# Gate tiles 10 and 11 as seven half-size products before the attention, instead of a plain product after it

## The reference, cut to what matters

```python
h = _rmsnorm(x, norm_g) * (1 + scale) + shift        # 512 x 1024
q_a,k_a,v_a,z_a,q_b,k_b,v_b,z_b,f_logit,g_logit = split(h @ w_in)
y_a = (stick_breaking(q_a,k_a,v_a) * silu(z_a)) @ w_o_sb
y_b = (forgetting_attention(q_b,k_b,v_b,F) * silu(z_b)) @ w_o_fox
gates = sigmoid(g_logit + b_gate)                    # 512 x 2048, 16 tiles of 128 features
x = x + gate * ((gates[:, :D] * y_a + gates[:, D:] * y_b) @ w_out)
```

## Time and profile before

| what | value |
|---|---|
| median of 3 runs | 1242.37 us |
| the profiled execution's own time | 1242.71 us |
| its span | 1240.9 us |
| PE / DVE / ACT / POOL busy | 98% / 69% / 53% / 35% |
| granted TensorE clock | 1.00 (2.4 GHz) in every stretch looked at |

### The profile page before, as it was taken

One profiled execution on the slowest core, in us unless ns is written; L12 is line 12 of the kernel. 1 busy time (PEld: TensorE's weight loads), 2 busy tenths in 40 slices (PEclk: granted clock), 3 DMA queues, 4 the chain that ended last, 5 costly groups with the idle time before them and its releaser, 6 DMA issues.

```text
span 1240.9 us, 22894 instructions
## 1 busy us (share of the span) xinstructions
PE 1213.3 (98%) x9270; PEld 1040.5 (84%) x9270; DVE 859.1 (69%) x1342; ACT 653.8 (53%) x1028; POOL 431.4 (35%) x330
## 2 busy tenths in 40 slices
PE   6999999999999999999998989999999999999999
PEld 6798999876767877777787768788878999999999
DVE  4289897789663266596648757456668888878974
ACT  6555463777665533463446544454335555556452
POOL 5562000422333736455343035540555223333000
PEclk9999999999999999999999999999999999999999
DMA  9953332666977993766321018851542565656554
GB/s 387 360 199 125 116 107 98 245 214 222 261 197 173 249 322 112 239 150 154 91 103 37 4 69 308 260 136 24 149 125 94 162 187 187 187 170 210 185 185 143
DMA packets 42182, 215.53 MB, mean 174 GB/s; under 512 B 5080, under 2 KB 5208, under 8 KB 28128
## 3 DMA queue, kind: packets, MB, share of 16 engines
q1 hardware_dynamic: 34272, 140.74, 32.2%
q0 software_dynamic: 4608, 28.31, 12.2%
q10 hardware_dynamic: 3200, 45.04, 9.8%
HBM read 206.72 MB, written 63.98 MB: 218 GB/s over the span
## 4 chain that ended last, share of the span: by engine, by line
PE 81%; DVE 9%; ACT 4%; POOL 2%; DMA 2%; issue 2%; ACTq 0%; SPq 0%; DVEq 0%; POOLq 0%
PE banks L663 79%; PE banks L670 2%; POOL weights_low L3281 2%; DMA weights<-in_stream 2%; DVE arena L2595 1%; DVE h_low L2336 1%; ACT weights_high L1487 1%; DVE arena L2592 1%; DVE arena L2597 1%; DVE weights_low L2336 0%; DMA arena<-in_mem 0%; POOL arena L3340 0%; ACT arena L1541 0%; DVE arena L2426 0%; DVE banks L2411 0%
## 5 line engine op out<-in xcount | busy, mean ns | idle before, releaser
L3281 POOL TENSOR_TENSOR weights_low<-weights,weights_high 128x512 fp32r<-128x512 f32 (+1 forms) x216 | 310.8, 1468 | 496.5 <-ACT weights_high L1487 496.5
L663 PE MATMUL banks<-h_high_low,weights_high 128*128 128x512 f32 (+1 forms) x696 | 243.3, 350 | 1.6 <-DVE h_low L2336 1.5
L663 PE MATMUL banks<-h_low,weights_high 128*128 128x512 f32 (+1 forms) x696 | 235.8, 339 | 0.0
L663 PE MATMUL banks<-h_high_low,weights_low 128*128 128x512 f32 (+1 forms) x696 | 235.8, 339 | 0.0
L1487 ACT ACTIVATE weights_high<-weights 128x2048 fp32r<-128x2048 f32 (+2 forms) x86 | 127.0, 1489 | 73.9 <-PE banks L663 58.4
L663 PEld LDWEIGHTS banks<-h_high_low,weights_high 128*128 128x128 f32 x696 | 131.2, 188 | 21.0 <-issue 3.0
L663 PEld LDWEIGHTS banks<-h_low,weights_high 128*128 128x128 f32 x696 | 131.1, 188 | 16.5 <-issue 2.4
L663 PEld LDWEIGHTS banks<-h_high_low,weights_low 128*128 128x128 f32 x696 | 131.1, 188 | 16.1
L663 PE MATMUL banks<-arena 64*64 64x64 f32 (+6 forms) x1800 | 116.6, 263 | 1.7 <-POOL arena L3340 0.7
L663 PEld LDWEIGHTS banks<-arena 64*64 64x64 f32 (+3 forms) x1800 | 84.8, 147 | 24.1 <-issue 17.0
L3359 POOL TENSOR_TENSOR weights_low<-weights,weights_high 128x512 fp32r<-128x512 f32 x32 | 48.5, 1537 | 112.6 <-ACT weights_high L1499 112.6
(11 more groups left out here) (463 smaller groups left out, 3293.2 us busy)
## 6 DMA issues: line engine op xcount, KB each, us to landing
weights<-in_stream SPq DMA_DIRECT2D x66, 1024.0 KB, 6.1
up_sums<-in_up POOLq DMA_DIRECT2D x16, 1024.0 KB, 9.5
weights<-up_sums SPq DMA_DIRECT2D x64, 256.0 KB, 2.9
weights<-in_up SPq DMA_DIRECT2D x48, 256.0 KB, 2.9
sums_kept<-in_down POOLq DMA_DIRECT2D x16, 704.0 KB, 7.7
arena<-in_ada SPq DMA_DIRECT2D x8, 1024.0 KB, 12.0
weights<-sums_kept SPq DMA_DIRECT2D x9, 704.0 KB, 4.1
sums_kept<-in_down ACTq DMA_DIRECT2D x8, 704.0 KB, 6.2
```

The source lines that it names most:

```text
L663: ins = nc.tensor.matmul(o, lhsT, rhs, start=start, stop=stop, skip_group_check=skip)
L3281: nc.gpsimd.tensor_tensor(lo_of(c)[:, cols], raw_of(c)[:, cols], hi_of(c)[:, cols].bitcast(F32), ALU.subtract).then_inc(sem("weights_split ...
```

## The change

One more early tile, gate pair 5 (tiles 10 and 11), is put between `za` and `qb`. It is written where `kb` will be, stored in `gates_kept` by ACT two tiles later, and loaded back at fox step 4 to where `va` was. Gate tiles 12 to 15 are now copied from `GATES_AT` to `sums` on the core (the accumulators of the norms, idle then) and read from there. Each wait on `keys_kept` counts one transfer more. `project("g", ...)` after the attention has no tiles left (`EARLY_G` 10). The second chunk of `va` is done like the first: blocks 0 and 1 side by side over k. The splitting of weights after the attention is placed after gates 9, 13 and 15; the DRAM copies are issued at every second m, and four of them in the next stage; the four lows of the `a` half of `gated` move into fox steps 5, 9, 13 and 17 on DVE. TensorE waits for `MOVED0` at step 2 instead of 1, and the bank order after the attention is 2, 3, 0, 1.

```diff
-EARLY_TILES = (("qa", 1), ..., ("za", 1), ("qb", 0), ("qb", 1), ("kb", 0), ("kb", 1), ("g", 6), ("g", 7))
+EARLY_TILES = (("qa", 1), ..., ("za", 1), ("g", 5), ("qb", 0), ("qb", 1),
+               ("kb", 0), ("kb", 1), ("g", 6), ("g", 7))
-Z_FIRST, EARLY_G = EARLY_TILES.index(("za", 0)), 12
+Z_FIRST, EARLY_G = EARLY_TILES.index(("za", 0)), 10
...
+        early_gates = {5: at(8192, 2, T), 6: at(GATES_AT, 2, T), 7: at(GATES_AT + 2 * T, 2, T)}
...
+            def values_in(c, n, ready=None):
+                slot, w = next_chunk(KD, n)
+                o = [M.take(pe, ("va", c, b)) for b in range(2)]
                 for k in range(KD):
+                    split_ready(k, KD)
...
+                    for b in range(2):
+                        mm3(o[b][:, 0:n], hrow(k, b), [p_[:, k, :] for p_ in w], k == 0, k == KD - 1, ...)
...
+            values_in(1, 256, h_ready(0))
             gate_rows_in(0, ADA_RING)
-            project_rows("va", 0, NB, hrow, NB, F_WIDE)
+            values_in(0, F_WIDE)
...
-                if i == 1:
+                if i == LAG:
                     pe.wait_ge(sem("product_moved"), MOVED0)
...
-                        M.use([0, 1, 2, 3])
+                        M.use([2, 3, 0, 1])
...
# ACT, early tiles, at R7
+                    if e >= 2 and EARLY_TILES[e - 2] == ("g", 5):
+                        act.wait_ge(sem("product_moved"), early_moved(e - 2, C12))
+                        act.dma_start(gates_kept, at(8192, 2 * T)).then_inc(sem("keys_kept"), 16)
# ACT, stick steps 1 and 2
-                    act.dma_start(gates_kept, at(GATES_AT, 4 * T)).then_inc(sem("keys_kept"), 16)
+                    act.dma_start(sums.rearrange("p a b -> p (a b)"), at(GATES_AT, 4 * T)).then_inc(sem("keys_kept"), 16)
-                    act.wait_ge(sem("keys_kept"), 48)
+                    act.wait_ge(sem("keys_kept"), 64)
# ACT, fox step 4
+                if i == 4:
+                    act.dma_start(at(512 * EARLY_G, 2 * T), gates_kept).then_inc(sem("keys_kept"), 16)
# ACT, after the attention
-            act.dma_start(at(GATES_AT, 4 * T), gates_kept).then_inc(sem("keys_kept"), 16)
             for m in range(SIDE_G, EARLY_G):
                 gate_out(m)
                 gate_inverse(m)
...
             for m in range(EARLY_G, 16):
+                if m == 14:
+                    split_weights()
+                src = gates[m] if m < 12 else sums[:, m - 12, :]
...
-            for _ in range(2):
-                split_weights()
+            split_weights()
             for m in range(KD):
                 act.wait_ge(sem("merged_raw"), m + 1)
                 high(merged_hi[m], merged_raw[:, m, :], sem("merged_hi"))
-                later_copies(S2, S1, m, 2)
+                if m % 2 == 0:
+                    later_copies(S2, S1, m // 2, 2)
                 if m % 4 == 3:
                     split_weights()
             def between_blocks(k):
+                if k < DOWN_PAIRS:
+                    later_copies(S2, S1, DOWN_PAIRS + k, 2)
# DVE
+                    if EARLY_TILES[e] == ("kb", 0):
+                        dve.wait_ge(sem("keys_kept"), 48)
...
+                if i % 4 == 1 and 5 <= i <= N + 1:
+                    gated_split(i // 4 - 1)
...
-            for m in range(8):
+            for m in range(4, 8):
```

More of the change, by code:

```diff
@@ L88 @@
 EARLY_FIRST = 11
-EARLY_TILES = (("qa", 1), ("ka", 0), ("ka", 1), ("za", 0), ("za", 1), ("qb", 0), ("qb", 1), ("kb", 0), ("kb", 1), ("g", 6), ("g", 7))
+EARLY_TILES = (("qa", 1), ("ka", 0), ("ka", 1), ("za", 0), ("za", 1), ("g", 5), ("qb", 0), ("qb", 1),
+               ("kb", 0), ("kb", 1), ("g", 6), ("g", 7))
 EARLY = len(EARLY_TILES)
-Z_FIRST, EARLY_G = EARLY_TILES.index(("za", 0)), 12
+Z_FIRST, EARLY_G = EARLY_TILES.index(("za", 0)), 10
 EARLY_STEPS = [[(c, f) for c, fs in ((i, (P1, R5)), (i - 1, (Q4, P3)), (i, (R7, P6, P2))) if 0 <= c < EARLY for f in fs]
@@ L344, in build @@
         GATES_AT = 10240
-        gates = [at(512 * m if m < EARLY_G else GATES_AT + 512 * (m - EARLY_G), T) for m in range(16)]
+        gates = [at(512 * m if m < 12 else GATES_AT + 512 * (m - 12), T) for m in range(16)]
+        early_gates = {5: at(8192, 2, T), 6: at(GATES_AT, 2, T), 7: at(GATES_AT + 2 * T, 2, T)}
         merged_raw, merged_lo = at(16384, 8, T), at_r("merged_low", 16384, 8, T)
@@ L556, in early_tile @@
             if key == "g":
-                return gates[2 * c + half][:, TH * side:TH * (side + 1)]
+                return early_gates[c][:, half, TH * side:TH * (side + 1)]
             to = {"qa": qa, "ka": ka, "za": gated["a"], "qb": qb, "kb": kb}[key]
@@ L824, in _ @@
             hrow = lambda k, b: (h_hi[:, k, P * b:P * (b + 1)], h_lo[:, k, P * b:P * (b + 1)])
[L825 to L834, removed]
-                for k in range(KD):
[L836 to L839, removed]
+            def values_in(c, n, ready=None):
+                slot, w = next_chunk(KD, n)
+                o = [M.take(pe, ("va", c, b)) for b in range(2)]
+                for k in range(KD):
+                    split_ready(k, KD)
+                    if ready is not None:
+                        ready(k)
+                    for b in range(2):
+                        mm3(o[b][:, 0:n], hrow(k, b), [p_[:, k, :] for p_ in w], k == 0, k == KD - 1,
+                            M.filled if k == KD - 1 else None)
+                for b in range(2, NB):
+                    o = M.take(pe, ("va", c, b))
+                    for k in range(KD):
+                        mm3(o[:, 0:n], hrow(k, b), [p_[:, k, :] for p_ in w], k == 0, k == KD - 1,
+                            M.filled if k == KD - 1 else None)
+                free_slot.append(slot)
+                chunk_end[-1] = ("va", c, NB - 1)
+            values_in(1, 256, h_ready(0))
             gate_bank = TR.take(pe, "gate")
@@ L1883, in _ @@
                 gate_inverse(m)
-            act.wait_ge(sem("keys_kept"), 64)
+            act.wait_ge(sem("keys_kept"), 80)
             for m in range(EARLY_G, 16):
-                link(nc.scalar.activation(gates[m], gates[m], ACT.Exp, scale=-1.0, bias=npar("b_gate", m)))
+                if m == 14:
+                    split_weights()
+                src = gates[m] if m < 12 else sums[:, m - 12, :]
+                link(nc.scalar.activation(gates[m], src, ACT.Exp, scale=-1.0, bias=npar("b_gate", m)))
                 inverse(gates[m]).then_inc(sem("gates"), 1)
-            for _ in range(2):
-                split_weights()
+            split_weights()
             for m in range(KD):
@@ L2605, in soft, with gated_split @@
                                                ALU.add, ALU.min, lowest).then_inc(M.out(key), 1)
+            def gated_split(m):
+                dve.wait_ge(sem("gated_hi"), m + 1)
+                low(gated_lo[:, m, :], gated_raw[:, m, :], gated_hi[m], sem("gated_split"))
             def mask_block(i):
@@ L2659, in _ @@
                     silu("b", 3)
-            for m in range(8):
-                dve.wait_ge(sem("gated_hi"), m + 1)
-                low(gated_lo[:, m, :], gated_raw[:, m, :], gated_hi[m], sem("gated_split"))
+            for m in range(4, 8):
+                gated_split(m)
             for m in range(KD):
@@ L3505, in lay_stream @@
         if i == 5:
-            parts.append(by_gates[EARLY_G // 2:])
-    parts.append(by_gates[:EARLY_G // 2])
+            parts.append(by_gates[6:])
+        if i == 3:
+            parts.append(by_gates[5:6])
+    parts.append(by_gates[:5])
     parts.append(lay_chunks(np.asarray(a["w_o_sb"])[0], 512))
@@ L3562 @@
     nF_kept = nc.dram_tensor("nF_kept", [HEADS, T], F32, kind="Internal").ap()
-    gates_kept = nc.dram_tensor("gates_kept", [P, 4 * T], F32, kind="Internal").ap()
+    gates_kept = nc.dram_tensor("gates_kept", [P, 2 * T], F32, kind="Internal").ap()
     sums_kept = nc.dram_tensor("sums_kept", [4, DOWN_PAIRS, P, DOWN_W], F32, kind="Internal").ap()
```

## The result

The changed kernel takes **1253.01 us** (median of 7, 1249.59 to 1259.25), the kernel before 1242.45 beside it (7 runs, 1241.44 to 1243.89): a ratio of **1.0094**, 95% interval 1.0077 to 1.011. It is slower, as forecast, and by 10.6 us where 6.25 was forecast; it lies 1 us above the range. The profiled execution of the changed kernel takes 1251.95 us of its own time, its span is 1250.2, the mean granted clock 0.997 (before: 1242.71, 1240.9, 1.000).

The account below looks back on a forecast made before the run. The prediction took TensorE as the bound. Terms -1.35, -0.4, +8.8 and -0.8 gave +6.25 on the profiled 1242.71, 1248.95, or 1248.6 us as median; its own range was 1245.5 to 1252, over the cases 1241 to 1252.

Parts of the forecast that it names:

- Part 1: Early tiles: gate tiles 10 and 11 move from plain products to one early tile of seven products, -1.35 us.
- Part 2: `va`: blocks side by side over k ask for the last low piece later, removing TensorE's wait, -0.4 us.
- Part 3: Gate tiles copied within SBUF to `sums`, and gate pair 5 loaded back at fox step 4: 0 us.
- rival (c): The copy within SBUF is slow: +5 us on top of the forecast, 1253.5 us, chance 0.08.
- Part 4: Lows made in fox steps, where DVE has room, and weight splits moved after the attention stay in time: 0 us.
- Part 5: POOL's last adds come one weight chunk later, so ACT's merging loop, DVE and TensorE wait before `wo`: +8.8 us.
- The prediction's worst case: Merging loop: each DVE step waits for a POOL piece of 1.4 us, twice a step; 8.8 would be about 11.
- Part 6: `wo`: with DRAM copies thinned out, the load starts before the first copy and TensorE's wait goes, -0.8 us.
- Nothing here rests on its changing: Clock: at 1.00, the 2.4 GHz level, in both windows read; the forecast does not depend on its changing.
- part 5's upper bound: Merging loop before `wo`: adds land at 451 and POOL disturbs DVE twice as much, +12.5 us.
- its +4.2: Lower bound at the merging loop before `wo`: adds land at 446.7 and POOL disturbs nothing, +4.2 us.

Follow-up runs that it names:

- the fastest version: The changed kernel with the DRAM copies and adds' wait moved into `wo`, lows in fox steps 7, 11, 15, 19, gates' load at step 11: 1240.07 us.

## Why the prediction was right in kind and short in size

**Part 1, gate pair by seven products: right.** Twelve tiles take 120.05 us, 10.0 each, and no gate tile is left for the 11.35 us: -1.4 for the -1.35 of the sum. DVE and ACT show no wait for the store.

**Part 2, `va` side by side: right.** From `va`'s last chunk to `qa` it is 11.81 us instead of 12.43: -0.6 for the -0.4 of the sum.

**Part 3: right on the copy within SBUF, wrong on the load.** The copy landed 4.8 us after its issue (5.6 to DRAM before), ACT no longer waits for it, and the early tiles do not stretch; rival (c) did not occur. But "a 0.5 MB one at fox step 4 is in its place, far from its use" looked at the load's own use only. It is issued on ACT's queue ahead of the forget rows, which DVE needs soon. The rows are from issues of the two traces (queue, KB, us from issue to landing), before and then after:

```profile
forget_rows<-nF_kept ACTq DMA_DIRECT2D x1, 512.0 KB, 13.2
```

```profile
arena<-gates_kept ACTq DMA_DIRECT2D x1, 512.0 KB, 12.2
forget_rows<-nF_kept ACTq DMA_DIRECT2D x1, 512.0 KB, 16.5
```

It lands 3.3 us later after its issue. The Trainium skill, DMA: Bandwidth & Descriptors, section Queues, rings and completion order, says that within one queue each DMA engine takes its work in ring order; these rows agree, and with the load at step 11 the wait is back at 3.9 us. The rest of the landing time is mostly the adds' traffic, as the 4.9 us with later adds show.

**Part 4: this step failed.** "Its four lows are made in fox steps, where DVE has room", at a cost of 0. DVE had room on the average, but in steps 5, 9, 13 and 17 the low stands in front of the scaling of the widest tile, 512 columns, and TensorE waited for the scaling of the weights behind the low, twice 0.53 us. With the load above, the attention took 174.28 us from the scores to its end instead of 172.89: **+1.4** where the prediction has 0. In the other two profiles of the changed kernel it is +4.1 and +1.7. The two weight splits, by contrast, were in time: TensorE has no wait in `oa` or at the start of `ob`.

**Part 5, the adds: the mechanism was right, the term too small.** The last pair was predicted 7.8 us after `ob`'s start and came at 7.7; ACT's release at +21.8 and came at +22.1. The end of the first `wo` tile was predicted 13.0 + 2.0 us after the release and came 16.3 after it. The loss is **10.4 where 8.8** was written. Of the 1.6 between, 0.3 is the release, and 0.6 lies between it and DVE's first low part (1.9 us where 1.3 was put down, since ACT first issues a DRAM copy). The steps behind took 0.4 more than written, and the last low with its matmuls 0.3. Within the steps, four of DVE's instructions beside POOL took 1.20, 1.77, 1.08 and 1.76 us instead of 0.69, 3.0 us more where 2.0 was put down, but the undisturbed steps were 1.94 us instead of 2.05.

The Trainium skill, SBUF — State Buffer, section SBUF: two separate sides, says that a DVE instruction with two SBUF inputs and a GpSimd instruction that reads SBUF lock each other out for the whole instruction. The rows agree: beside POOL every DVE instruction with both inputs in SBUF is long, and the one that reads a PSUM bank (461.17) takes its usual 0.68. The prediction's worst case, a whole piece of about 1.4 us for each of them, did not come: the four waited 0.4 to 1.1.

**Part 6, the thinned copies: right.** The wait at 463 is gone. The kernel before is 1.2 us over an unhindered `wo` stage, where 0.8 was forecast.

**The sum by the first profile.** Early tiles, `va` and attention leave `oa` 0.43 late where -1.75 was forecast. Of the 2.2 between, 1.4 is parts 3 and 4, -0.2 part 2, and 1.05 is a last chunk of `va` that began at 87.19 instead of 86.14. TensorE already lags by 0.7 us some 10 us into the span, before anything that the change touches. Over all thirteen profiles this chunk begins between 86.14 and 87.89, and latest in the fastest version, so I take the 1.05 for a difference between executions. Then 0.1 up to `ob`, +10.4, -1.2, and -0.55 behind `wo`, which is such a difference too: +9.2 of the span's +9.3. Forecast were +6.25, so 3.0 are missing by the profile, 1.6 in part 5 and 1.4 in parts 3 and 4; the rest of the stages and the two differences between executions nearly cancel. The other 1.3 us of the 10.6 come from comparing medians: the changed kernel's is 1.1 above its profiled execution. "Nothing here rests on its changing" was said of the clock, and that failed as well: of the three profiles, one has a half-clock stretch in `wo` that cost 1.5 us, and forget rows 2.66 us late for TensorE. How often that happens in the executions without a profile stays open.

**Why the range was too narrow.** Its upper end, 1252, is little more than part 5's upper bound alone (12.5 instead of 8.8 gives 1252.3); no cost in the attention could be added to it, since parts 3 and 4 had no upper end of their own beyond rival (c). An own bound for "the low stands in front of the scaling" (DVE's 0.69 us in each of four steps, 2.8 us) was there to be had. The lower end doesn't follow from part 5 at all: its +4.2 gives 1244.0, not 1245.5.

## What to carry to other kernels

A wait costs what is queued behind it, not what it guards: one wait for adds, placed in ACT's queue in front of work that feeds DVE and TensorE, made 10.4 us, and moving it by one loop gave all of it back with the adds as late as ever. When work is taken out of a schedule, look which later steps counted their place in it (here POOL's adds count weight chunks), and for each load moved, what stands behind it in the same queue. An engine's mean share does not say that it has room in the step in which one puts something.

## What the runs showed of the chip

- TensorE's granted clock fell to half while it stood 4.95 us: matmuls of 512 columns were 0.43 us apart from 454.5 to 458.9 instead of 0.235. That was free of charge, since DVE set the pace. A second such stretch in another execution of the same kernel, where TensorE was the bound, cost 1.5 us.
- Beside POOL's pieces DVE's instructions with two inputs in SBUF took 1.08 to 1.77 us instead of 0.69; the one that reads a PSUM bank took 0.68 as always.
- The wait for a late add pair is very steady: ACT's was 16.39 to 16.65 us in all six profiles that have it. The landing of a 0.5 MB load in a queue with another ahead of it isn't: DVE waited 6.7 to 9.4 us in three of the same kernel.
- A pair of adds (2 x 704 KB) lands 14.4 us after its issue under load, twice the 7.2 us of engine time worked out from the earlier trace rows.
- From 450 to 452, while all engines waited for the adds, the DMA engines moved only 41 GB/s, against 307 in the 4 us before: the last of such a wait is not bytes on full DMA engines.
- A copy of 1 MB within SBUF landed 4.8 us after its issue, one of the same source to DRAM 5.6.
